# Hybrid encoder layer on eight cores: when second-FFN weights, a reload, an addition and output weights are issued, and the last block in column parts

## The reference

```python
gates = jax.nn.sigmoid(gate_logits + b_gate).reshape(B, S, N_BRANCHES, D)
merged = gates[:, :, 0] * y_conv + gates[:, :, 1] * y_attn + gates[:, :, 2] * y_mem
x = layer_norm(DEEPNORM_ALPHA * x + merged @ w_o, ln1_g, ln1_b)

gate, up = jnp.split(x @ w_ffn_in, 2, axis=-1)
ffn = (jax.nn.silu(gate) * up) @ w_ffn_out
return layer_norm(DEEPNORM_ALPHA * x + ffn, ln2_g, ln2_b)
```

## Time and profile before

| | |
|---|---|
| median of 3 runs | 1008.57 us (1007.62 to 1011.27) |
| profiled execution | 1010.17 us, its longest span 1009.1 us (core 1) |
| spans of the eight cores | 995.7 to 1009.1 us |
| PE busy on core 1 | 962.5 us (95%) |
| DVE, ACT, POOL busy | 549.9, 407.7, 286.3 us |
| line 1166, addition from PSUM, 128x512 | 132 instructions, 684 ns each |
| line 1173, product, 128x512 | 66 instructions, 1350 ns each |
| line 1050, bias addition, 128x1024 | 16 instructions, 2539 ns each |
| line 808, last step of the fold, 128x512 | 44 instructions, 470 ns each |
| line 1023, square with sum, 128x1024 | 32 instructions, 1058 ns each |
| first-FFN weight loads | 44 of 512 KB, 3.7 us to landing (median) |
| second-FFN weight loads | 22 of 256 KB, 6.4 us to landing (median) |

### The profile page before, as it was taken

One profiled execution on the slowest core, in us unless ns is written; L12 is line 12 of the kernel. 1 busy time (PEld: TensorE's weight loads), 2 busy tenths in 40 slices (PEclk: granted clock), 3 DMA queues, 4 the chain that ended last, 5 costly groups with the idle time before them and its releaser, 6 DMA issues.

```text
span 1009.1 us, 16357 instructions; the slowest of 8 cores (995.7 to 1009.1 us)
## 1 busy us (share of the span) xinstructions
PE 962.5 (95%) x5606; PEld 449.3 (45%) x5606; DVE 549.9 (54%) x903; ACT 407.7 (40%) x653; POOL 286.3 (28%) x296
## 2 busy tenths in 40 slices
PE   4999999989899999999999999999999999999996
PEld 1455544544444444444445444444444444444442
DVE  0324576657563222222458698776475577763554
ACT  1135566657462222222244456445222345443221
POOL 3200000202134334333321234444333134333321
PEclk9999999999899999999999999999999999999998
DMA  9997134554339999911067045786433322220232
GB/s 129 168 174 137 24 88 106 73 116 69 59 64 135 135 145 130 155 56 70 1 188 272 34 130 146 176 184 146 147 125 125 125 84 84 85 84 1 84 107 81
DMA packets 39392, 112.11 MB, mean 111 GB/s; under 512 B 4944, under 2 KB 16856, under 8 KB 38192
## 3 DMA queue, kind: packets, MB, share of 16 engines
q0 software_dynamic: 11104, 41.16, 27.7%
q1 hardware_dynamic: 28208, 69.91, 21.6%
HBM read 132.49 MB, written 30.47 MB: 161 GB/s over the span
## 4 chain that ended last, share of the span: by engine, by line
PE 84%; DMA 8%; DVE 3%; issue 2%; ACT 1%; SPq 1%; POOL 0%; DVEq 0%; ACTq 0%; POOLq 0%
PE ps L233 83%; DMA arena<-w_out 2%; DMA arena<-w_bf_cache 2%; DMA arena<-w_q 1%; DMA arena<-xt 1%; SPq L147 1%; DMA arena<-u_scratch 1%; DMA gexp_scratch<-arena 1%; PE ps L1109 1%; DVE arena L1166 1%; DVE arena L1045 0%; DVE arena L1041 0%; POOL arena L147 0%; ACT arena L597 0%; PE ps L688 0%
## 5 line engine op out<-in xcount | busy, mean ns | idle before, releaser
L233 PE MATMUL ps<-arena 128*128 128x512 bf16 (+5 forms) x5196 | 946.5, 362 | 36.2 <-DMA arena<-xt 16.5
L233 PEld LDWEIGHTS ps<-arena 128*128 128x128 bf16 (+2 forms) x5196 | 428.8, 98 | 536.2 <-issue 81.7
L837 DVE SCALAR_TENSOR_TENSOR arena<-arena,ps 128x512 f32<-128x512 f32 x96 | 65.9, 686 | 146.6 <-PE ps L233 142.7
L1173 POOL TENSOR_TENSOR arena<-arena 128x512 bf16<-128x512 f32 x66 | 89.1, 1350 | 155.8 <-DVE arena L1166 155.2
L816 ACT ACTIVATE arena<-ps,bgate_sb 128x512 f32<-128x512 f32 x96 | 66.0, 688 | 166.2 <-PE ps L233 166.2
L1163 ACT COPY arena<-ps 128x512 f32<-128x512 f32 x132 | 76.9, 587 | 137.2 <-PE ps L233 137.2
L1166 DVE TENSOR_TENSOR arena<-arena,ps 128x512 f32<-128x512 f32 x132 | 88.2, 684 | 39.5 <-PE ps L233 39.0
L844 POOL TENSOR_TENSOR arena<-arena 128x512 f32<-128x512 f32 x32 | 40.8, 1274 | 125.4 <-DVE arena L837 125.4
L1023 ACT ACTIVATE arena<-arena 128x1024 bf16<-128x1024 f32 x32 | 33.8, 1058 | 93.3 <-DVE arena L1285 82.1
L147 POOL DMA_DIRECT2D arena<-w_g x21 | 11.3, 544 | 169.2 <-PE ps L233 168.1
L1045 DVE SCALAR_TENSOR_TENSOR arena<-arena,rs 128x1024 bf16<-128x1024 f32 (+1 forms) x32 | 56.1, 1752 | 1.7
(11 more groups left out here) (103 smaller groups left out, 450.1 us busy)
## 6 DMA issues: line engine op xcount, KB each, us to landing
arena<-w_bf_cache SPq DMA_DIRECT2D x44, 512.0 KB, 3.7
arena<-u_scratch SPq DMA_DIRECT2D x64, 135.0 KB, 3.4
arena<-x SPq DMA_DIRECT2D x16, 512.0 KB, 10.5
y_scratch<-arena SPq DMA_DIRECT2D x16, 512.0 KB, 3.2
arena<-y_scratch SPq DMA_DIRECT2D x16, 512.0 KB, 3.5
out<-arena SPq DMA_DIRECT2D x16, 512.0 KB, 2.6
arena<-w_f POOLq DMA_DIRECT2D x22, 256.0 KB, 6.4
arena<-w_g POOLq DMA_DIRECT2D x9, 512.0 KB, 12.8
```

The source lines that it names most:

```text
L233: return pe.run(lambda: nc.tensor.matmul(out, lhsT, rhs, start=start, stop=stop, skip_group_check=onto), deps, inc)
L837: t_y = dve.run(lambda: nc.vector.scalar_tensor_tensor(out=gb[r], in0=gb[r], scalar=1.0, in1=ps[:, bk, :], op0=ALU.add, op1=ALU.mult), [tk ...
L1173: return pool.run(lambda: nc.gpsimd.tensor_tensor(out=dst, in0=up, in1=gate, op=ALU.mult), deps)
```

## The change

Five things move; the arithmetic is the same. The output weights of pairs 1 to 3 are issued after the first of the three gate loads instead of after the last. The second-FFN weights are issued one per unit, from unit 0 to unit 21. The reload for block 10 moves from block 7's row steps to unit 32. Block 8's `hb_prep`, its scaling and its addition on GpSimd, moves from unit 32 to behind the second pass's drain. The last block, 15, is computed by a new function in column parts of 512, 256 and 256; row sum and square are taken over 768 columns and 256 columns, the row steps and the store over two halves.

```diff
         for b in range(3):
             t_wg[dp, b] = load(wgs[r][:, b], w_g_d[:, dp, b], deps)
-
-    def load_wos(dp, deps):
-        t_wo_[dp] = load(wos[dp % 2], w_out_d[:, dp], deps)
+            if b == 0:
+                t_wo_[dp] = load(wos[r], w_out_d[:, dp])
...
         load_wg(1, [[t_sT[3, c] for c in range(4)]])
-        load_wos(1, [])
...
+    def f2_last(tb):
+        c0 = (tb % 8) * 128
+        r = tb % 3
+        xb = HB[r]
+        b, dO = banks.alloc(2)
+        b3, d3 = banks.alloc(1)
+        out = [bank2(b)[:, 0:512], bank2(b)[:, 512:768], ps[:, b3, 0:256]]
+        st, mv = stt[:, tb % 4, :], mvt[:, tb % 4, :]
+        tok = []
+        for i, (lo, n) in enumerate(((0, 512), (512, 256), (768, 256))):
+            for j in range(22):
+                tk = mm(out[i], actT[j][:, c0:c0 + 128], w2[j][:, lo:lo + n], j == 0, j == 21,
+                        [dO, d3, a_tok[j, 1]] if i == 0 else (), inc=(j == 21))
+            tok.append(tk)
+        sm = [hsum[:, 1, tb:tb + 1], mv[:, 3:4]]
+        sq = [st[:, 1:2], st[:, 2:3]]
+        parts = [(0, 768), (768, 1024)]
+        t_sq = []
+        for i, (lo, hi) in enumerate(parts):
+            t_h = dve.run(lambda: nc.vector.scalar_tensor_tensor(
+                out=xb[:, lo:hi], in0=xb[:, lo:hi], scalar=ALPHA, in1=bank2(b)[:, 0:768] if i == 0 else out[2], op0=ALU.mult, op1=ALU.add,
+                accum_out=sm[i]), [tok[1 + i], hb_x[tb]])
+            t_sq.append(act.run(lambda: nc.scalar.activation(junk[:, lo:hi], xb[:, lo:hi], AF.Square, accum_out=sq[i]), [t_h]))
+        t1 = dve.run(lambda: nc.vector.tensor_scalar(
+            out=mv[:, 0:1], in0=sm[0], scalar1=sm[1], scalar2=1.0 / D, op0=ALU.add, op1=ALU.mult), [t_h])
...
+        t_rs = ln_rstd(t3, tb, rs16[:, 16 + tb:17 + tb])
+        t_y = [ln_center(xb[:, lo:lo + 512], ln2t[0][:, lo:lo + 512], tb, [t_sq, t1]) for lo in (0, 512)]
+        for i, lo in enumerate((0, 512)):
+            t_ln = ln_scale(xb[:, lo:lo + 512], xb[:, lo:lo + 512], rs16[:, 16 + tb:17 + tb], ln2t[1][:, lo:lo + 512], [t_rs, t_y[i]])
+            dma(sp, out_d[tb * 128:(tb + 1) * 128, lo:lo + 512], xb[:, lo:lo + 512], s_out[r], [t_ln])
...
-            load_hb(tb + 3)
+            if tb != 7:
+                load_hb(tb + 3)
...
-        if u >= 8:
-            for _ in range(2):
-                if w2_order:
-                    load_w2(w2_order.pop(0))
+        load_w2(u)
...
+            if tb == 15:
+                f2_last(tb)
+                break
...
                 if u == 32:
-                    hb_prep(8)
+                    load_hb(10)
             f1_drain(43, 8)
+            hb_prep(8)
```

More of the change, by code:

```diff
@@ L964, in _build @@
     load_wg(2, [pe.tok()])
-    load_wos(2, [])
     cache_w1(4)
@@ L968, in _build @@
     load_wg(3, [pe.tok()])
-    load_wos(3, [])
     t_wo = load(w_o_sb, w_o_d, [a_done])
@@ L1279, in f2_mm @@
         return bO, tk
+    def f2_last(tb):
[23 more added lines that the diff above has]
+            out=mv[:, 0:1], in0=sm[0], scalar1=sm[1], scalar2=1.0 / D, op0=ALU.add, op1=ALU.mult), [t_h])
+        t2 = dve.run(lambda: nc.vector.scalar_tensor_tensor(
+            out=mv[:, 1:2], in0=mv[:, 0:1], scalar=mv[:, 0:1], in1=eps_t[:, 0:1],
+            op0=ALU.mult, op1=ALU.subtract), [t1, t_eps])
+        t3 = dve.run(lambda: nc.vector.tensor_scalar(
+            out=st[:, 3:4], in0=sq[0], scalar1=sq[1], scalar2=1.0 / D, op0=ALU.add, op1=ALU.mult), t_sq)
+        t3 = dve.run(lambda: nc.vector.tensor_tensor(out=mv[:, 1:2], in0=st[:, 3:4], in1=mv[:, 1:2], op=ALU.subtract), [t2, t3])
+        t_rs = ln_rstd(t3, tb, rs16[:, 16 + tb:17 + tb])
[3 more added lines that the diff above has]
+            dma(sp, out_d[tb * 128:(tb + 1) * 128, lo:lo + 512], xb[:, lo:lo + 512], s_out[r], [t_ln])
     def f2_block(tb, hooks={}):
@@ L1348, in _build @@
             d_chain(tb - 6, 8, 16)
-    w2_order = list(range(22))
     for u in range(22):
@@ L1368, in _build @@
     f1_drain(21, 0)
-    assert not w2_order
     load_w1(24)
```

## The result

The changed kernel took 997.15 us (median of five executions, 995.70 to 1001.43) beside 1008.32 us for the kernel before (median of four, 1007.62 to 1011.27). The ratio is 0.989, with a 95% interval of 0.986 to 0.992. The profiled execution took 996.51 us. The prediction was 996.5 us, from 993 to 1002, and faster.

The account below looks back on a forecast made before the run. TensorE's stops and the end after its last matmul bound the kernel; on core 1, 4.2 + 1.7 + 1.5 + 1.5 + 2.0 + 1.7 + 1.6 = 14.2 us off 1009.1 gives 994.9. With 1.1 outside and 0.5 for short stops: 996.5 us, range 993 to 1002.

Parts of the forecast that it names:

- The bound: Whole kernel: time can come only from places where TensorE stops and from the end after its last matmul.
- Second-FFN loads: First FFN pass, core 1: one load per unit removes 4.2 us of waits and 1.7 us of clock.
- The limit: First-FFN load in a store unit: may take up to 6.1 us before TensorE sees it; 4.7 us expected.
- Rival 1: Some store units: first-FFN loads still late, one 4.0 us stop remains on the slowest core; 1000.5 us, chance 0.15.
- Rival 2: All seven store units: one second-FFN load makes each late, seven stops of 4.0 us; 1024.5 us, chance 0.03.
- Reload: Start of second pass: with block 10's reload in unit 32, the first-FFN load leaves 2.7 us earlier; 1.5 us gained.
- Addition: Unit 32: TensorE's 1.46 us stop goes; behind the drain block 8's addition is hidden by 1.8 us.
- Rival 4: Behind the second pass's drain: the moved addition reaches TensorE, 1.5 us back; 998 us, chance 0.04.
- Output weights: Gate stretch near 321 us, core 1: issued second, their 2.0 us wait and 1.7 us of clock go.
- rival 3: Gate stretch: output weights' wait becomes one for the third gate load, 3.7 us back on core 1; 999.7 us, chance 0.05.
- The end: After the last matmul: last block in column parts saves 1.6 us, bounds -0.6 and 3.0.
- row sum and square: Last block: shrinking both from 1024 to 256 columns saves 0 to 1.7 us, 1.2 taken.

Follow-up runs that it names:

- the kernel with the scaling in unit 32: Changed kernel, but block 8's ScalarE scaling back in unit 32, only its GpSimd addition behind the drain; 997.32 us, single execution.
- the kernel with whole rows: Changed kernel, but last block's centring, scaling and store over all 1024 columns again; 998.62 us, single execution.
- single loads alone: Kernel before with one edit, second-FFN weights one load per unit from unit 0; 1006.69 us, ratio 0.997.
- the kernel with pairs in odd units: Changed kernel, but second-FFN loads in pairs at the ends of odd units, beside the store of y; 1000.29 us, ratio 0.993.

## Why the prediction was right, step by step

**The bound.** Right: the time came from places where TensorE stopped, and its unbroken stretches stayed as they were. Core 1 was forecast at 994.9 us and took 994.9: its back fell by 10.9 us (4.2 + 1.7 + 1.5 + 1.5 + 1.6 = 10.5 forecast), its front by 3.3 (3.7 forecast). The forecast did not say that the next slowest core would be drawn by the front. Core 5, forecast at 994.4, took 991.0, and core 2, which the sum left out, 995.5. That the total came within 0.7 us of the measured time is therefore in part luck: the fronts spread by several us from one execution to the next, and core 1's own was 510.6 us in the first trace of the changed kernel and 501.4 in the second.

**Second-FFN loads.** The limit held: 6.1 us on core 1, 6.1 to 6.4 us in nearly all such units of all traces. The latency that was set against it was too small. 4.7 us was the middle of two medians over units with and without a store, while the limit concerns units with one. The median of 4.4 us on core 1 after the change mixes them too: its loads behind a store took 4.9, 5.8 and 6.1 us, the other five 3.3 to 4.9. The last of the three used up nearly all of the 1.3 us that a fold may wait (core 1's timeline):

```profile
657.69 0.79 DVE L805 TENSOR_TENSOR arena<-arena 128x1024 bf16<-128x1024 bf16 x1 [1.23 <-DMA arena<-w_bf_cache]
```

So the stops went as forecast on core 1, but with less than 0.1 us to spare and not with 1.4. Rival 1 (stops that get rarer without vanishing) did occur, in small: 0.5 to 1.5 us of waits on four cores in the profiled execution, and in the five other traces with the same loads and stores 0.2 to 6.3 us over eight cores, the longest stop 1.4 us. One sign that was named for being wrong came as well: folds that wait in units 1 to 7. They did so on cores 2, 3 and 5 of the changed kernel, by up to 1.5 us, and TensorE stopped there for 1.4 us on one core of the kernel with the scaling in unit 32, for 1.2 us on one of the kernel with whole rows, and for 2.26 and 1.93 us with single loads alone. The store units that got a load for the first time were thus clear on most cores and not, as the forecast had it, on all. The Trainium skill ("DMA: Bandwidth & Descriptors", "Queues, rings and completion order") has the DMA engines take turns between queues; the traces agree that a first-FFN load is slower beside converting loads (8.7 us and 5.2 us by when the pair goes out).

Rival 2 (all store units late) did not occur. Price of a stop: in the kernel with pairs in odd units, cores 3 and 6 waited 3.7 and 2.8 us in line 1162 and have backs 5.3 and 4.8 us longer than the undisturbed ones, so about 1.6 to 2.0 us beside the waits; each has one stretch of 3.4 us at the lower level, 1.7 us as taken. Not every stop pays it: of the 16 stops of 1.5 us or more in line 1166 in the kernel before, 5 are followed by such a stretch.

**Reload.** Right in size and cause: the stop of 1.51 us is gone, and the kernel with the reload behind unit 24 shows that SyncE's standing was the cause.

**Addition.** Right: 1.46 us gone, nothing in its place. The first addition of the pair behind the drain ends at about 917.34 + 4.65 / 2 = 919.7, the row sum that needs it starts at 921.56, so it is hidden by 1.9 us, 1.8 forecast. Rival 4 did not occur.

**Output weights.** The wait is gone, and rival 3 (a wait for the third gate load) did not occur: the median gate load went from 10.1 to 16.8 us and TensorE did not see it. The trace bears out the term of 3.7 us on core 1; device time of the kernel with that order undone does not, either way.

**The end.** The mechanism was right and the size a little off: 2.1 us where 1.6 was taken, inside the bounds of -0.6 and 3.0. The mis-sized term is that of row sum and square: 1.9 us where 1.2 was taken and 1.7 was the bound, because two small steps left the chain with them. The halves lost 0.4 us in operations (0.3 taken) and gained 0.6 in the store (0.7 taken), and the narrower matmuls cost 0.05 (zero taken). The 1.1 us of the kernel with whole rows look like the 1.2 taken but are not the same thing: they are the 1.9 less what GpSimd's late small step costs there.

## What to carry to other kernels

When a load that a matmul stream depends on is late only sometimes, read off how much lateness is absorbed (latency less stop), and judge every edit to other traffic by whether it pushes the load past that limit: when other loads go out, and what waits ahead of it in its own queue, did more here than how much was moved. A DMA with a long wait should not stand ahead of an urgent one in an in-order queue. And with several cores, compare stretches behind an event common to all of them; the slowest core's span mixes the edit with whatever made that core late.

## What the runs showed of the hardware that was not expected

GpSimd's step on 128x1 elements (line 1033, line 1037 before) is the same instruction in three kernels and took three times. Before, it took 0.55 us at the end of the program, issued at 1003.57, 0.04 us after VectorE's centring had started. In the changed kernel centring on 512 columns had started 0.23 us ahead of it, and it took 0.93; with whole rows, centring on 1024 columns had started 0.23 us ahead, and it took 1.46. In the last two cases it ended about 0.4 us after the VectorE instruction that was running when it started.

The step runs 256 times in each of the fourteen traces, on eight cores, and so tests this by itself. Where it started 0.06 to 0.23 us behind a VectorE instruction with both inputs in SBUF, 424 times, it took 0.90 to 1.63 us and ended 0.40 to 0.43 us after that instruction. Where VectorE had for 0.07 to 0.6 us been running an instruction that reads one of its inputs from PSUM, 1182 times, it took 0.55 to 0.57 us, as it does with VectorE idle. Core 1 before the change, where the row sum had started 0.24 us ahead:

```profile
517.09 1.22 DVE L1070 SCALAR_TENSOR_TENSOR arena<-arena,ps 128x1024 f32<-128x1024 f32 x1 [1.87 <-PE ps L233]
517.33 0.57 POOL L1037 TENSOR_TENSOR rs<-mvt,eps_t 128x1 f32<-128x1 f32 x1
```

So in these cases GpSimd was held until a VectorE instruction with two SBUF inputs was over, and not by one that reads PSUM. The Trainium skill ("SBUF — State Buffer", "SBUF: two separate sides") says that, of a GpSimd operation that reads SBUF and a VectorE operation with two SBUF inputs, the one that starts first keeps the shared ports for its whole instruction. The traces agree in both directions: VectorE's 0.42 us step became 2.38 beside GpSimd's addition in unit 32, and here a GpSimd step of half a microsecond became one and a half. They do not agree at the closest starts: 1472 times the step started 0.04 us behind centring on 1024 columns, as at the end of the program before, and took 0.55 us all the same. What decides there is open.
